# Where in their buffers the weight chunks and the operands of the products begin

## What is computed

```python
y = swiglu(modulate(x, ...), ffn_w13[l, 0], ffn_w2[l, 0])      # x @ w13: "up"; (...) @ w2: "down"
x = layer_norm(ALPHA * x + 0.5 * (1 + mod[:, 0, 2])[:, None, :] * y, ...)
y = token_mixer(modulate(x, ...), w_in[l], w_out[l], ...)       # x @ w_in: "up"; (...) @ w_out: "down"
...
mkv = (mem @ w_mem_kv)                                          # keys and values of the memory, made first
u = depthwise_conv_centred(x @ w_up, conv_w, conv_b)
ffn = (jax.nn.silu(gate) * val) @ w_down
```

## The kernel before

| form | moving at | stationary at | moving minus stationary |
|---|---|---|---|
| upward | 480 | 160 | 320 |
| tokens | 160 | 480 | 192 |
| stage 0, both forms | 160 | 160 | 0 |
| downward, feed-forward | 160 | 160 | 0 |
| downward, mixer | 160 | 480 | 192 |

## Time and profile before

### The profile page before, as it was taken

The page is one execution under the profiler, slowest core; times in us unless marked ns, Lnnn a source line. Parts: engine busy times, 40 slices in busy tenths (PEclk is TensorE's granted clock), DMA queues, the critical chain, the costliest instruction groups (busy, mean ns, idle before and its releaser), DMA issues.

```text
span 2101.3 us, 39270 instructions
## 1 busy us (share of the span) xinstructions
PE 2002.5 (95%) x16744; PEld 1854.1 (88%) x16744; DVE 1575.3 (75%) x2135; ACT 1073.1 (51%) x1516; POOL 308.4 (15%) x247
## 2 busy tenths in 40 slices
PE   7999989999999999899999999898999997989998
PEld 7999879979998998789889989887899887979996
DVE  6688788766987677688675649886788489758874
ACT  4543365455434443564554435565665375646652
POOL 0200032111000200203011004610120036002100
PEclk9999999999999999999999999899999999999999
DMA  9888743335985677443245663233465533324552
GB/s 378 325 315 330 279 161 132 106 120 203 354 340 205 243 284 303 148 163 122 82 173 207 252 226 118 101 141 115 147 202 193 205 125 141 122 101 161 202 199 80
DMA packets 60381, 409.85 MB, mean 195 GB/s; under 512 B 6896, under 2 KB 6896, under 8 KB 13872
## 3 DMA queue, kind: packets, MB, share of 16 engines
q1 hardware_dynamic: 54000, 384.85, 49.4%
q0 software_dynamic: 5920, 22.07, 3.1%
q10 hardware_dynamic: 288, 0.42, 0.1%
HBM read 404.17 MB, written 3.15 MB: 194 GB/s over the span
## 4 chain that ended last, share of the span: by engine, by line
PE 76%; DVE 14%; ACT 4%; POOL 2%; issue 2%; DMA 2%; SPq 0%; DVEq 0%; POOLq 0%; ACTq 0%
PE ps L713 13%; PE ps L714 13%; PE ps L715 13%; PE ps L757 7%; PE ps L759 6%; PE ps L758 6%; DVE l L601 4%; PE ps L742 2%; PE ps L1725 2%; PE ps L744 2%; PE ps L743 2%; DMA w<-in_stream 2%; PE ps L625 1%; DVE tmp L975 1%; ACT h L586 1%
## 5 line engine op out<-in xcount | busy, mean ns | idle before, releaser
L601 DVE TENSOR_TENSOR l<-w,h 128x2048 fp32r<-128x2048 f32 (+1 forms) x295 | 672.7, 2283 | 150.1 <-ACT h L586 149.7
L713 PE MATMUL ps<-xh,h 128*128 128x256 f32 x2544 | 722.3, 284 | 19.3 <-DVE gq L2423 9.4
L586 ACT CAST h<-w 128x2048 fp32r<-128x2048 f32 (+1 forms) x295 | 557.0, 1893 | 331.4 <-PE ps L759 162.1
L714 PE MATMUL ps<-xl,h 128*128 128x256 f32 x2544 | 713.6, 281 | 0.0
L715 PE MATMUL ps<-xh,l 128*128 128x256 f32 x2544 | 712.9, 280 | 0.0
L713 PEld LDWEIGHTS ps<-xh,h 128*128 128x128 f32 x2544 | 480.4, 189 | 27.6 <-DVE l L601 12.3
L714 PEld LDWEIGHTS ps<-xl,h 128*128 128x128 f32 x2544 | 480.3, 189 | 2.4 <-issue 2.4
L715 PEld LDWEIGHTS ps<-xh,l 128*128 128x128 f32 x2544 | 480.1, 189 | 0.0
L757 PE MATMUL ps<-h,hh 128*128 128x512 f32 x528 | 207.4, 393 | 0.0
L759 PE MATMUL ps<-h,hl 128*128 128x512 f32 x528 | 205.6, 389 | 0.0
L758 PE MATMUL ps<-l,hh 128*128 128x512 f32 x528 | 205.5, 389 | 0.0
(11 more groups left out here) (425 smaller groups left out, 3007.1 us busy)
## 6 DMA issues: line engine op xcount, KB each, us to landing
w<-in_stream SPq DMA_DIRECT2D x361, 1024.0 KB, 4.9
GB<-in_vec POOLq DMA_DIRECT2D x20, 512.0 KB, 5.8
w<-in_stream SPq DMA_DIRECT2D x8, 512.0 KB, 4.1
gate<-in_vec POOLq DMA_DIRECT2D x6, 512.0 KB, 4.0
memf<-in_memT SPq DMA_DIRECT2D x2, 512.0 KB, 6.1
xf<-in_xT POOLq DMA_DIRECT2D x1, 1024.0 KB, 9.5
kv<-mk POOLq DMA_DIRECT2D x2, 512.0 KB, 6.1
kv<-mv POOLq DMA_DIRECT2D x2, 512.0 KB, 8.6
```

Of the source, the lines that this page charges most:

```text
L586: e.copy(k.H[m % NH][:, 0:z], k.W[n % NW][:, 0:z]).then_inc(k.hi_done, 1)
L601: e.tensor_tensor(k.L[m % NH][:, 0:z], k.W[n % NW][:, 0:z], k.H[m % NH][:, 0:z], SUB).then_inc(k.lo_done, 1)
L713: p.matmul(P[:, 0:T], H[:, r, o], xh[:, r, :], start=r == 0, stop=False)
L714: p.matmul(P[:, 0:T], H[:, r, o], xl[:, r, :], start=False, stop=False)
```

## The change

`H` and `L` begin at multiples of 512 and get 512 bytes of slack each; `XH`, `XL` and what is placed with them, and the base of the inner activations, come to multiples of 512 too; stage 0's activations are stacked 448 bytes above the base. A table gives each stage an offset in bytes, and the upward chunks of the stage are written and read that far into their `H` and `L` buffers. Downward chunks stay at 0. The `W` buffers do not move. No instruction is added or taken away, no wait and no order is changed.

```diff
+        self.at = (self.at + 511) // 512 * 512
+        self.H = [keep(f"h{i}", [128, CH + 128], F32R) for i in range(NH)]
+        self.L = [keep(f"l{i}", [128, CH + 128], F32R) for i in range(NH)]
+        x = self.top = (self.top - 7 * 4096) // 512 * 512
...
+        k = self.stack(self.base + 448, memf=[128, 8, T], xf=[128, 8, T], eh=[128, 8, T], el=[128, 8, T], ftmp=[128, 8, T])
...
+SHIFT = [0, 64, 64, 192, 320, 192, 448, 64, 64, 320, 192]
+INTO = [0 if MATS[m][0] in DOWN else SHIFT[s] // 4 for s in range(len(STAGES)) for m in chunk_of(s)]
+
+def part(b, m, z):
+    return b[m % NH][:, INTO[m]:INTO[m] + z]
...
-            e.copy(k.H[m % NH][:, 0:z], k.W[n % NW][:, 0:z]).then_inc(k.hi_done, 1)
+            e.copy(part(k.H, m, z), k.W[n % NW][:, 0:z]).then_inc(k.hi_done, 1)
...
-            e.tensor_tensor(k.L[m % NH][:, 0:z], k.W[n % NW][:, 0:z], k.H[m % NH][:, 0:z], SUB).then_inc(k.lo_done, 1)
+            e.tensor_tensor(part(k.L, m, z), k.W[n % NW][:, 0:z], part(k.H, m, z), SUB).then_inc(k.lo_done, 1)
...
-        v = lambda b: rr(b[:, 0:8 * n], "p (k n) -> p k n", k=rows)
-        return v(k.H[m % NH]), v(k.L[m % NH])
+        v = lambda b: rr(part(b, m, 8 * n), "p (k n) -> p k n", k=rows)
+        return v(k.H), v(k.L)
```

More of the change, by code:

```diff
@@ L380, in buffers @@
         self.W = [keep(f"w{i}", [128, CH]) for i in range(NW)]
-        self.H = [keep(f"h{i}", [128, CH], F32R) for i in range(NH)]
-        self.L = [keep(f"l{i}", [128, CH], F32R) for i in range(NH)]
-        x = self.top = self.top - 7 * 4096
+        self.at = (self.at + 511) // 512 * 512
+        self.H = [keep(f"h{i}", [128, CH + 128], F32R) for i in range(NH)]
+        self.L = [keep(f"l{i}", [128, CH + 128], F32R) for i in range(NH)]
+        x = self.top = (self.top - 7 * 4096) // 512 * 512
         self.XH, self.XL = self.place("xh", [128, 8, T], x, F32R), self.place("xl", [128, 8, T], x + 8192, F32R)
@@ L399, in buffers @@
         assert f["end"] <= self.ln_at, (f["end"], self.ln_at)
-        k = self.stack(self.base, memf=[128, 8, T], xf=[128, 8, T], eh=[128, 8, T], el=[128, 8, T], ftmp=[128, 8, T])
+        k = self.stack(self.base + 448, memf=[128, 8, T], xf=[128, 8, T], eh=[128, 8, T], el=[128, 8, T], ftmp=[128, 8, T])
         self.memf, self.xf, self.eh, self.el, self.ftmp = (k[n] for n in ("memf", "xf", "eh", "el", "ftmp"))
```

## The result

The changed kernel takes 2091.69 us (median of five executions, 2082.16 to 2095.59) against 2105.43 us; the ratio is 0.9935, with a 95% interval of 0.9918 to 0.9953. It is faster, by 13.7 us where 35 were forecast. Its profiled execution has a span of 2082.7 us, 18.6 less than the 2101.3 of before.

The account below looks back on a forecast made before the run. TensorE's long row of matmuls was taken as the bound behind stage 0. Gains of 26.9 + 4.7 + 2.8 + 0.9 + 0.5 = 35.8 us gave 2070 us, range 2038 to 2108.

Parts of the forecast that it names:

- The bound: Behind stage 0 the kernel is one long row of TensorE matmuls; the time between starts counts.
- The price of an upward row: Upward in six feed-forwards: 6048 matmuls go from 117.8 to 113.3 ns, gaining 26.9 us.
- Mixers: In mixers: upward 4.7 us, downward 2.8, tokens 0.9 in dense tiles and 0.5 in opening tiles gained.
- Downward in feed-forwards, stage 0, feed: Downward keeps distance 0, stage 0 is held by DMA: no gain; stage 1's stream rises to about 312 GB/s.
- The 32 bytes matter: All operands: alignment to 64 bytes saves one piece per read, a further 25 us, 2045 us; chance 0.20.
- Placement isn't the cause: All rows: differing prices come from what ran before a tile or from the form; 2105 us; chance 0.10.
- Slower, near 0: Stages 1, 2, 6, 7, 8: distances 64 and 448 cost 120.0 ns like distance 0; 2114 us; chance 0.14.
- Only the distance counts, by its old prices: Stages 3, 5, 10 keep 117.8 ns, 1, 2, 6, 7, 8 perhaps too; 2097 us; chance 0.14.
- the case of no effect: Whole kernel: time the same as before, within 0.3% or 6.3 us; chance 0.15.

Follow-up runs that it names:

- the two kernels of one class each: Changed kernel with upward and tokens distances behind stage 0 all 192 modulo 256: 2083.95 us, ratio 0.9908; or all 64 modulo 256: 2103.00 us, ratio 1.0003.
- the three mixed kernels: Kernel with all rows at 192 modulo 256, upward L moved 128 bytes from H; tokens likewise, unmixed, or the other way round: 2079.25, 2079.37, 2078.85 us.

## Why the prediction was right and wrong

**The bound: right.** TensorE's row of matmuls set the time; each feed-forward that fell to 113.3 ns became 4.4 to 4.5 us shorter, as 1008 x 4.45 ns says, and nothing became late behind it: in stage 1 DMA went to 311 GB/s as worked out.

**The price of an upward row: the step that failed.** The prediction saw that the trace has two prices at the very same addresses, said that distance alone doesn't fix them, and then took 113.3 for all 6048. (A third price, the 117.2 of the earlier trace rows, is 117.8: the timeline gives hundredths of a us, which is 0.6 ns on one of 18 matmuls.) By the count of rows, stages 1, 4 and 8 (class 192) draw it 7 times in 10 and stages 3, 6 and 10 (class 64) once in 10: 3 x 0.72 + 3 x 0.09 = 2.4 feed-forwards of 4.5 us, 10.9 us, instead of six and 26.9. That count takes short and long rows alike. By tiles of feed-forwards alone, the same eight profiles have 600 of 672 at 113.3 in class 192 and 170 of 1134 in class 64, which makes 3.1 feed-forwards and 14.0 us. The changed kernel's three profiles have 168, 72 and 126 of 252 tiles at 113.3: 4.0, 1.7 and 3.0 feed-forwards. What was missing could have been counted in the trace of before: nearly all upward rows, at 320, ran at 117.8, and most tokens rows, at 192, at 113.3. I took that for luck that any odd multiple would have. In that trace alone class and form can't be told apart; the two kernels of one class each show that it was the class modulo 256, and half of the table of offsets, 192 and 448, keeps upward rows in the bad one.

**Mixers: mis-sized.** 4.7 + 2.8 + 0.9 + 0.5 us were counted; the four mixers changed by -0.6 us in the profiles. The prices came as forecast (226.7 downward; 11 of 16 dense upward tiles of stage 2 at 113.3) except upward in stage 5, which is in class 64 and stayed at 117.8 in all but one tile, and tokens, which in stages 2, 7 and 9 went from mostly 113.3 to mostly 117.8, being now in class 64. But these prices don't show in the length of the mixers. The four together took 848.3 us before. In the three mixed kernels, where all upward rows have 113.3 and all downward ones 226.7, they took 846.4, 849.0 and 845.6 us: the 4.7 + 2.8 us that the prediction counted for just these prices come to somewhere between -1 and 3 us. What else ends the waits there no run took apart. The lengths also move with the clock: stage 2 got longer at a granted clock of 0.96 instead of 0.98, and stage 7 shorter at 0.97 instead of 0.94, here before and after:

```profile
1280.10:1497.90 217.80, 198.95 (x1633) 180.61 (x1633) 171.65 (x251) 130.30 (x216) 63.46 (x44) 0.94 0.36 127
...
1273.10:1488.60 215.50, 193.57 (x1633) 176.23 (x1633) 171.64 (x251) 130.23 (x216) 63.30 (x44) 0.97 0.36 128
```

**Downward in feed-forwards, stage 0, feed: right**, at nothing. Downward stayed at 226.7. Stage 0 stayed at the DMA's pace (67.0 us, 375 GB/s), though its rows came to 117.8 from 120.0.

**The rivals.** "The 32 bytes matter" fell with the kernel that moved just these. "Placement isn't the cause" fell with the two classes, 19 us apart. The Trainium skill, on the page "SBUF — State Buffer" (section "Who interferes with whom"), says that TensorE's two read ports are independent and that it never waits on anyone. The trace doesn't agree with that as a guide to the pace of a row: 113.3 to 120.0 ns, by where its own two operands lie. That the ports are the reason no run shows. "Slower, near 0" fell: 64 and 448 give 113.3 or 117.8, never 120. "Only the distance counts, by its old prices", 2097 us, came nearest in time, but not in kind: it had stages 3, 5 and 10 fixed at 117.8, and stage 10 ran at 113.3 in one execution and at 117.8 in the next.

**The time and the range.** 2091.7 lies in 2038 to 2108, but that range takes in the case of no effect, so its holding says little. The single forecast, 2070, was 22 us too low: 13 to 16 us by the upward term (26.9 counted, 14.0 or 10.9 by the two counts above), the rest by the mixers' 8.9 us, of which nearly nothing came. The time of one execution isn't one number here: the change spreads over 19 us and the kernel before over 2087 to 2110, and the share of each trace's long rows at 113.3 differs from execution to execution.

## What to carry to other kernels

In rows of matmuls that each load 128 columns of 32-bit weights, read the pace from start to start, and if it stands above columns per clock, vary the distance between moving and stationary operand modulo 256: here it moved 256 columns between 113.3 and 120.0 ns and 512 columns between 226.7 and 234.3. One trace of such a kernel shows one draw; where two prices appear at equal addresses, count the rows at each by class before a price is put into a sum, and look for a placement under which the dear one can't last, which gave 12 us more and took the spread from 19 us in 13 executions to between 3 and 8 in five or six.

## What the runs showed of the hardware

- Four of the prices are whole multiples of 6.67 ns, which is 16 columns at 2.4 GHz: 113.3 is 17, 120.0 is 18, 226.7 is 34, 233.3 is 35 of them. 117.8 is 53 for three matmuls; others, such as 118.7, 231.1 and 232.4, fit only over more matmuls or not at all, so that one step lies behind all of them isn't shown. At half clock the extra is gone.
- Two paces are stable at one placement. A row that begins nearly always keeps the one it falls into, for a thousand matmuls (stage 8 once at 113.3 and once at 117.8 for all 42 tiles); two tokens rows went from 113.3 to 117.8 midway. What at the begin decides between them wasn't tried.
- The distance counts modulo 256 bytes, but for 1 ns between 128 and 384 downward. Adding 32 bytes to both operands changes no price; a distance off the multiples of 64 costs 118.3 to 120.0 ns upward and 233.3 to 234.3 downward.
- A round of three matmuls has a price that isn't the sum of its pairs' prices. With `L` 128 bytes from `H`, `H` in class 192 and `L` in class 64 leave only 113.3 to upward rows, and the other order gives 118.9.
